# A two-layer decoder step: squares summed on TensorE, the root taken from PSUM, smaller residual chunks and stores

## The reference

```python
def rmsnorm(x, g):
    y = x * lax.rsqrt(jnp.mean(x * x, axis=-1, keepdims=True) + RMS_EPS)
    return y * g

def layer(x, g_pre, g_post, w_in, w_o, ...):
    h = rmsnorm(x, g_pre)
    ... = jnp.split(h @ w_in, SPLITS, axis=-1)      # mixer inputs, memory queries, gate
    o = jnp.concatenate([o_tok, o_mem], axis=-1)
    y = (o * jax.nn.silu(gate)) @ w_o
    return x + rmsnorm(y, g_post)
```

## Time and profile before

| | |
|---|---|
| time, three runs | 1710.7, 1711.69, 1712.37 us; median 1711.69 |
| profiled execution, its own time | 1713.43 us |
| its span, first to last instruction | 1711.8 us |
| busy: PE, DVE, ACT, POOL | 1623.2, 1049.7, 401.3, 160.8 us |
| mean granted TensorE clock | 0.981 of 2.4 GHz |
| transfers | 419.95 MB |

### The profile page before, as it was taken

How to read it: one execution, slowest core, us unless ns; L and a number is a source line. 1 busy time by engine, 2 the same in 40 slices (tenths; PEclk the granted TensorE clock), 3 DMA queues, 4 the chain that set the end, 5 groups by cost and what they waited for, 6 DMA issues and landing times.

```text
span 1711.8 us, 27852 instructions
## 1 busy us (share of the span) xinstructions
PE 1623.2 (95%) x9596; PEld 1285.7 (75%) x9596; DVE 1049.7 (61%) x4973; ACT 401.3 (23%) x1002; POOL 160.8 (9%) x295
## 2 busy tenths in 40 slices
PE   7999999899999999989989989999999999999995
PEld 6677776677777777657977867777777777888895
DVE  4887546746465555437872467777777777431755
ACT  2131111101121212211111433333333333221011
POOL 1121112112111121220000000000000000020000
PEclk9999999999999999999999999999999999999998
DMA  9689999999999999995433233333333323374441
GB/s 384 235 335 415 411 406 395 384 396 420 405 401 422 417 419 412 366 379 239 148 141 149 103 101 102 103 103 102 103 109 103 103 78 118 111 272 176 148 148 52
DMA packets 101725, 419.95 MB, mean 245 GB/s; under 512 B 41796, under 2 KB 46288, under 8 KB 91984
## 3 DMA queue, kind: packets, MB, share of 16 engines
q0 software_dynamic: 41680, 218.91, 32.1%
q1 hardware_dynamic: 53256, 187.54, 28.9%
q10 hardware_dynamic: 6648, 11.73, 1.8%
HBM read 405.28 MB, written 12.85 MB: 244 GB/s over the span
## 4 chain that ended last, share of the span: by engine, by line
PE 76%; DVE 9%; ACT 6%; DMA 5%; issue 2%; POOLq 0%; POOL 0%; ACTq 0%; DVEq 0%; SPq 0%
PE psum L743 25%; PE psum L1171 11%; PE psum L812 10%; PE psum L794 6%; PE psum L1034 5%; DMA kvr<-in_cv 3%; PE psum L732 3%; PE psum L781 2%; PE psum L1218 2%; DMA kvr<-in_ck 1%; PE psum L1228 1%; PE psum L754 1%; ACT gT L1777 1%; PE psum L769 1%; DVE kvr L1939 1%
## 5 line engine op out<-in xcount | busy, mean ns | idle before, releaser
L1939 DVE CUSTOM_DVE_ANT_0 kvr<-kvr,arena 128x128 f32<-128x128 f32 x1488 | 323.6, 285 | 114.4 <-DMA kvr<-in_ck 114.0
L743 PE MATMUL psum<-hT,wring 128*128 128x264 f32 x1536 | 364.8, 394 | 0.0
L743 PEld LDWEIGHTS psum<-hT,wring 128*128 128x128 f32 x1536 | 291.9, 194 | 67.8 <-issue 19.8
L1171 PE MATMUL psum<-hT,kvr 128*128 128x264 f32 x1152 | 283.0, 391 | 1.8 <-DVE hT L2267 1.8
L1171 PEld LDWEIGHTS psum<-hT,kvr 128*128 128x128 f32 x1152 | 213.5, 191 | 42.3 <-issue 8.9
L794 PE MATMUL psum<-hT,kvr 128*128 128x264 f32 x512 | 121.5, 388 | 0.0
L1939 DVE DVE_READ_ACCUMULATOR2_ANT arena<- 128x1 f32 x1488 | 120.2, 81 | 0.0
L794 PEld LDWEIGHTS psum<-hT,kvr 128*128 128x128 f32 x512 | 94.8, 190 | 15.8 <-issue 0.9
L677 POOL DMA_DIRECT2D kvr<-in_cv x128 | 67.7, 529 | 377.9 <-PE psum L1034 288.2
L1034 PE MATMUL psum<-kvr,arena 128*32 128x384 f32 x1024 | 98.8, 502 | 4.5 <-DMA kvr<-in_cv 4.5
L677 POOL DMA_DIRECT2D kvr<-in_ck x128 | 67.6, 528 | 216.7 <-issue 216.7
(11 more groups left out here) (433 smaller groups left out, 2318.5 us busy)
## 6 DMA issues: line engine op xcount, KB each, us to landing
kvr<-in_ck POOLq DMA_DIRECT2D x128, 768.0 KB, 11.8
kvr<-in_cv POOLq DMA_DIRECT2D x128, 768.0 KB, 11.4
kvr<-in_wrkv SPq DMA_DIRECT2D x12, 3072.0 KB, 11.9
kvr<-in_wo SPq DMA_DIRECT2D x14, 2048.0 KB, 8.3
wring<-in_wkv SPq DMA_DIRECT2D x12, 2048.0 KB, 11.8
wring<-in_wm SPq DMA_DIRECT2D x8, 2048.0 KB, 12.5
wring<-in_wg SPq DMA_DIRECT2D x8, 2048.0 KB, 12.0
kvr<-in_wg SPq DMA_DIRECT2D x8, 2048.0 KB, 8.8
```

Source lines behind the costliest of these rows:

```text
L743: last = mm(psum[:, m % 2, 0:n], w[:, k, t * P:(t + 1) * P], rhs[:, k, 0:n], start=(k == 0), stop=(k == KT - 1))
L1171: last = mm(psum[:, m % 2, 0:T], w[:, k, t * P:(t + 1) * P], hT[:, k, :], start=(k == 0), stop=(k == KT - 1))
L1939: last = v_.tensor_tensor_reduce(page, page, qb[:, n % 2, h * P:(h + 1) * P], 1.0, 0.0, ALU.mult, ALU.add, S[:, n % 2, j * FH + h:j * FH + ...
```

## The change

- **Squares.** DVE adds the squares of rows j = 0 to 13 only. PE adds the accumulator and the last two squares, straight from ACT's buffers, in one accumulation over three ones-products (`n_sq` counts the two squares). This holds in both layers.
- **Root.** ACT takes the root from PSUM with scale 1/D and a bias of RMS_EPS from the new tile `eps`; DVE takes the reciprocal after it, not before. A Sqrt of one column ahead of row 14 loads ACT's function table there. `rsx` now lies in `acc0`.
- **Joint.** `residual` runs over eight chunks of 1, 1, 2, 2, 2, 4, 2 and 2 rows; the weighted sums of row 15 come after the fifth. ACT counts `h_out` for every row, and PE waits for every row. The other three ones-products follow LoRA's row 13. LoRA writes banks 6 and 7, so queries 0 and 1 wait for no LoRA eviction. `hT` is scaled by `inv2` quarter by quarter as PE has read it for the last query (`q_read`), ahead of that query's eviction.
- **End.** PE puts rows 0 to 6 of `xT` into seven banks by an identity product and adds the scaled rows of `oT` to them; ACT copies the sums back. DVE only scales these rows and does both passes for rows 7 to 15. SP issues seven stores of 2, 2, 3, 3, 3, 2 and 1 rows in that order.

Left out of the diff: the weight buffers of the late products count on the semaphores `g_full` instead of `u_full` (with matching numbers).

```diff
@@ -273,6 +273,7 @@
+        eps = sb("eps", [P, 2])
@@ -373,7 +374,7 @@
-        rsx = sq0[:, 0, :]
+        rsx = acc0
@@ -462,15 +463,23 @@
+        RESIDUAL = [(0, 1), (1, 2), (2, 4), (4, 6), (6, 8), (8, 12), (12, 14), (14, 16)]
+        SUMS_LEFT = 5
+        ADDED = [(0, 2, True), (2, 4, True), (4, 7, True), (7, 10, False), (10, 13, False), (13, 15, False), (15, 16, False)]
+        ADD_BANKS = (0, 1, 3, 4, 5, 6, 7)
 @@ -604,7 +613,7 @@
             unit(I["wqm1"], 1, 0)
-            sp.wait_ge(sem("h_out"), 16)
+            sp.wait_ge(sem("h_out"), 28)
             for j in range(2):
@@ -657,6 +666,11 @@
                 late_unit(v)
+            x_added, x_out = 0, 0
+            for k0, k1, on_pe in ADDED:
+                x_added, x_out = (x_added + k1 - k0, x_out) if on_pe else (x_added, x_out + 1)
+                sp.wait_ge(*(sem("x_added"), x_added) if on_pe else (sem("x_out"), x_out))
+                sp.dma_start(O["yT"][:, k0 * T:k1 * T], xT[:, k0:k1, :].rearrange("p k t -> p (k t)")).then_inc(sem("stored_y"), 16)
@@ -755,20 +769,21 @@
-            def lora_tiles(after):
+            def lora_tiles():
                 pe.wait_ge(sem("w_full0"), 32)
-                for t in range(2):
-                    pe.wait_ge(sem("p_free"), M_LORA + t + 1)
+                pe.wait_ge(sem("y_out"), 2 * FEW0)
                 for k in range(KT):
-                    if k % 4 == 0:
-                        pe.wait_ge(sem("h_out"), after + k // 4 + 1)
+                    pe.wait_ge(sem("h_out"), 8 + k + 1)
                     for t in range(2):
-                        m = M_LORA + t
                         w = wring[:, 0, t * KT * LORA:(t + 1) * KT * LORA].rearrange("p (k n) -> p k n", k=KT)
-                        last = mm(psum[0:LORA, m % 2, 0:T], w[:, k, :], hT[:, k, :], start=(k == 0), stop=(k == KT - 1))
+                        last = mm(psum[0:LORA, 6 + t, 0:T], w[:, k, :], hT[:, k, :], start=(k == 0), stop=(k == KT - 1))
                         if k == KT - 1:
                             last.then_inc(sem("p_done"), 1)
+                    if k == KT - 3:
+                        for n, (out, total) in enumerate(((B, accg), (Wp, accx), (Xp, accxx))):
+                            pe.wait_ge(sem("n_acc"), min(n + 4, 5))
+                            mm(out[:, 0:T], ones, total, start=True, stop=True).then_inc(sem("n_ss"), 1)
@@ -776,9 +791,11 @@
                     w = wring[:, slot, :].rearrange("p (k n) -> p k n", k=KT)
-                    pe.wait_ge(sem("p_free"), m + 1)
+                    pe.wait_ge(sem("p_free"), m + 1 if t >= 2 else M_LORA + 2)
                     for k in range(KT):
                         last = mm(psum[:, m % 2, 0:T], w[:, k, t % 2 * P:(t % 2 + 1) * P], hT[:, k, :], start=(k == 0), stop=(k == KT - 1))
+                        if t == 3 and k in (3, 7, 11):
+                            last.then_inc(sem("q_read"), 1)
                     last.then_inc(sem("p_done"), 1)
@@ -1139,10 +1156,13 @@
                 few_products(i)
-            for n, (out, total) in enumerate(((A, acc0), (B, accg), (Wp, accx), (Xp, accxx))):
-                pe.wait_ge(sem("n_acc"), min(n + 3, 5))
-                mm(out[:, 0:T], ones, total, start=True, stop=True).then_inc(sem("n_ss"), 1)
-            lora_tiles(8)
+            pe.wait_ge(sem("n_acc"), 3)
+            mm(A[:, 0:T], ones, acc0, start=True, stop=False)
+            for n in range(2):
+                pe.wait_ge(sem("n_sq"), 2 + n + 1)
+                last = mm(A[:, 0:T], ones, sq0[:, n, :], start=False, stop=n == 1)
+            last.then_inc(sem("n_ss"), 1)
+            lora_tiles()
             memory_queries()
@@ -1166,7 +1186,7 @@
                     if o == -2 and t == 0:
-                        pe.wait_ge(sem("h_out"), 12 + n + 1)
+                        pe.wait_ge(sem("h_out"), 24 + n + 1)
                     for k in range(4 * (n % 4), 4 * (n % 4) + 4):
@@ -1389,7 +1409,18 @@
             pe.wait_ge(sem("n_acc"), 6)
-            mm(A[:, 0:T], ones, acc1, start=True, stop=True).then_inc(sem("n_ss"), 1)
+            mm(A[:, 0:T], ones, acc1, start=True, stop=False)
+            for n in range(2):
+                pe.wait_ge(sem("n_sq"), 4 + n + 1)
+                last = mm(A[:, 0:T], ones, sq1[:, n, :], start=False, stop=n == 1)
+            last.then_inc(sem("n_ss"), 1)
+            pe.wait_ge(sem("y_out"), 2 * (FEW0 + 8))
+            for n, bank in enumerate(ADD_BANKS):
+                mm(psum[:, bank, 0:T], ident, xT[:, n, :], start=True, stop=False)
+            for n, bank in enumerate(ADD_BANKS):
+                chunk = [k0 <= n < k1 for k0, k1, _ in ADDED].index(True)
+                pe.wait_ge(sem("y_normed"), chunk + 1)
+                mm(psum[:, bank, 0:T], ident, oT[:, n, :], start=False, stop=True).then_inc(sem("p_done"), 1)
@@ -1423,7 +1454,9 @@
                     act.wait_ge(sem("sq_used"), nth - 1)
-                ac(sq[:, j % 2, :], oT[:, n, :], ACT.Square)
+                last = ac(sq[:, j % 2, :], oT[:, n, :], ACT.Square)
+                if j >= 14:
+                    last.then_inc(sem("n_sq"), 1)
                 ac(oT[:, n, :], oT[:, n, :], ACT.Copy, scale=gpost(layer)[:, n:n + 1]).then_inc(sem("p_free"), 1)
@@ -1628,16 +1661,16 @@
             for n in range(16):
+                if n == 14:
+                    ac(eps[:, 1:2], eps[:, 1:2], ACT.Sqrt)
                 output_tile(0, n)
+            act.wait_ge(sem("n_ss"), 3)
+            ac(rsx, A[:, 0:T], ACT.Sqrt, scale=1.0 / D, bias=eps[:, 0:1]).then_inc(sem("n_rt"), 1)
+            for n, (k0, k1) in enumerate(RESIDUAL):
+                act.wait_ge(sem("x_new"), n + 1)
+                for k in range(k0, k1):
+                    ac(hT[:, k, :], xT[:, k, :], ACT.Copy, scale=gpre(1)[:, k:k + 1]).then_inc(sem("h_out"), 1)
             act.wait_ge(sem("n_ms"), 3)
-            ac(rsx, inv2, ACT.Sqrt).then_inc(sem("n_rt"), 1)
-            for c in range(4):
-                act.wait_ge(sem("x_new"), c + 1)
-                for k in range(4 * c, 4 * c + 4):
-                    last = ac(hT[:, k, :], xT[:, k, :], ACT.Copy, scale=gpre(1)[:, k:k + 1])
-                last.then_inc(sem("h_out"), 1)
-            act.wait_ge(sem("n_ms"), 4)
             ac(inv2, inv2, ACT.Sqrt).then_inc(sem("n_rt"), 1)
@@ -1794,13 +1827,15 @@
             for n in range(16):
+                if n == 14:
+                    ac(eps[:, 1:2], eps[:, 1:2], ACT.Sqrt)
                 output_tile(1, n)
-            root(4, rs1)
-            for c in range(4):
-                act.wait_ge(sem("x_out"), c + 1)
-                act.dma_start(O["yT"][:, 4 * c * T:(4 * c + 4) * T], xT[:, 4 * c:4 * c + 4, :].rearrange("p k t -> p (k t)"))\
-                    .then_inc(sem("stored_y"), 16)
-            act.wait_ge(sem("stored_y"), 64)
+            act.wait_ge(sem("n_ss"), 7)
+            ac(rs1, A[:, 0:T], ACT.Sqrt, scale=1.0 / D, bias=eps[:, 0:1]).then_inc(sem("n_rt"), 1)
+            for n, bank in enumerate(ADD_BANKS):
+                act.wait_ge(sem("p_done"), M_WO1 + 16 + n + 1)
+                ac(xT[:, n, :], psum[:, bank, 0:T], ACT.Copy).then_inc(sem("x_added"), 1)
+            act.wait_ge(sem("stored_y"), 16 * len(ADDED))
             act.wait_ge(sem("stored_lf"), 16)
@@ -2105,7 +2140,7 @@
                     joined(i)
-                for j in (14, 15):
+                for j in () if layer else (14,):
                     output_sums(layer, j)
@@ -2127,12 +2162,15 @@
                 s, total = (sq0, sq1)[layer][:, j % 2, :], (acc0, acc1)[layer]
-                last = v_.tensor_copy(total, s) if j == 0 else tt(total, total, s, ALU.add)
+                if layer or j < 14:
+                    last = v_.tensor_copy(total, s) if j == 0 else tt(total, total, s, ALU.add)
                 if layer:
...
                     dve.wait_ge(sem("sq_used"), nth + 1)
+                    if j == 13:
+                        dve.sem_inc(sem("n_acc"), 1)
                     return
-                if j == 15:
+                if j == 13:
                     last.then_inc(sem("n_acc"), 1)
@@ -2150,12 +2188,13 @@
-            def residual(c, buf):
-                rows4 = slice(4 * c, 4 * c + 4)
-                ch.do(tt(oT[:, rows4, :], oT[:, rows4, :], buf.unsqueeze(1).to_broadcast([P, 4, T]), ALU.mult))
-                return tt(xT[:, rows4, :], xT[:, rows4, :], oT[:, rows4, :], ALU.add)
+            def residual(k0, k1, buf):
+                rows_ = slice(k0, k1)
+                ch.do(tt(oT[:, rows_, :], oT[:, rows_, :], buf.unsqueeze(1).to_broadcast([P, k1 - k0, T]), ALU.mult))
+                return tt(xT[:, rows_, :], xT[:, rows_, :], oT[:, rows_, :], ALU.add)
+            v_.memset(eps[:, :], RMS_EPS)
             quad, total = oT[:, 0:4, :], oT[:, 4:8, :]
@@ -2223,16 +2262,16 @@
-            dve.wait_ge(sem("n_ss"), 3)
-            ch.do(ts(inv2, A[:, 0:T], 1.0 / D, RMS_EPS, ALU.mult, ALU.add))
-            v_.reciprocal(inv2, inv2).then_inc(sem("n_ms"), 1)
```

(44 more changed lines are left out.)

## The result

The changed kernel took 1698.27 us, the median of five runs (1692.97 to 1701.55), and the kernel before 1710.7 in the five runs beside them (1706.42 to 1712.37). The ratio is 0.9922 with a 95% interval of 0.9902 to 0.9941: **13.3 us faster (10.1 to 16.8)**, where the prediction had 10.7. Applied to the 1710.7 of the same runs, the ratio gives 1697.4, a hair under the range's low end of 1697.5. The direction was right, and so were the terms of the two edited places; the gain came out 2.6 larger than forecast, although 10.7 still lies inside the interval.

The account below looks back on a forecast made before the run. PE carries three quarters of the chain; changes off it pay only where PE stands still. Joint 6.7 plus end 4.0 gave 10.7 off the 1711.69 median: 1701.0 us, range 1697.5 to 1706.5.

Parts of the forecast that it names:

- the terms of the two edited places: Between the layers and at the kernel's end: 6.7 and 4.0 us saved, sum 10.7.
- The joint: Between the layers: LoRA's earlier end 4.5, no eviction wait 0.45, hT scaling hidden 1.75; sum 6.7 us.
- that case: LoRA between the layers: the clock returns to full rate more slowly, costing 1.7 us.
- The end: Last rows: earlier reciprocal 1.41, less DVE work 1.77, smaller last store 0.85; sum 4.0 us.
- Two signs of being wrong: Clock at 0.50 past 896 in LoRA; third SP store issued after the fourth's rows are ready.
- Rival 1: LoRA between the layers: PE pauses between rows and stays at half rate; net 3.4 us slower, 1715; chance 0.06.
- Rival 2: Turn loop waits for something not shifted, so the joint's gain stays there and only the end pays: 1707.7; chance 0.09.
- Rival 3: At the end, PE at half rate makes the additions hold up the stores: net 5.2 us faster, 1706.5; chance 0.09.
- Rival 4: Table reload costs 0.9 at each root, one or two further half-rate stretches in the turn loop: 1709 to 1712; chance 0.06.
- The step that failed: Turn loop from 945 to 1693: the joint's shift of 6.7 us runs through unchanged.
- the half rate in the first turn: Stretch after 987 in the turn loop: its absence, worth 3.2 us, served to widen the range.

Follow-up runs that it names:

- fill: Changed kernel plus eight unread products of ones in PE's pause ahead of LoRA; one run, joint gains 0.05 us.
- the joint alone: Changed kernel with the end of the kernel before; r at 51.35 against 58.13 us, loop 747.30.
- the end alone: Kernel before with only the end changed; end 14.49 against 18.40 us, loop 751.04.
- last three: Changed kernel with its last two stores made one of three rows; DVE done 0.26 us earlier, span ends 0.20 later.
- DVE adds all: Changed kernel with DVE doing both passes for all sixteen rows at the end; the additions on PE and ACT are worth 2.4 to 2.5 us.
- turn filler: Changed kernel plus five unread products in PE's waits in the first turn; first turn 1.63 us shorter, loop 746.65 against 746.37.
- all three: Changed kernel plus unread products ahead of LoRA and in the first turn, and row 15's sums later; ratio 0.9903 to the kernel before.
- sums late: Changed kernel with only row 15's weighted sums two chunks later on DVE; one run, queries 0.58 us later.
- no early load: Changed kernel without the one-column Sqrt ahead of row 14, both layers; 1698.22 us in a single run, 0.9 lost in each place.
- chunks of four: Changed kernel with the residual in four chunks of four rows, row 15's sums after the second; queries start at 25.81, 2.94 us later.
- fill and sums late: Changed kernel plus eight unread products ahead of LoRA and row 15's sums two chunks later; ratio 0.9930 to the kernel before.
- scaled after: Changed kernel with hT scaled after the last query's eviction, as before; queries to r 30.43 us instead of 28.48.

## Where the prediction held, and the step that failed

**The joint held, term by term.** Counted from the mark: PE's sum of row 15 ended at 1.53 (forecast 1.62), the reciprocal began at 2.13 (2.07), LoRA at 5.56 (5.45), queries at 22.87 (22.7), r at 51.35 (51.4). Two small errors cancelled: the queries started 4.76 earlier than before, not 4.95, and from there to r it took 2.02 less, not 1.75 (removing the scaling was worth 1.95 by itself). The root from PSUM took 0.49, not the 0.39 of the earlier trace rows; unlike that one it reads a column, the bias. That the column is the reason was not tested, but ACT's copies that read a column of `gvec` took 0.50 beside 0.42 for its squares, which read none. The prices of two- and three-row passes (0.15 + 0.277 per row) came out at 0.70 and 0.97 as worked out. There is some luck in the agreement: with the longer fall, which two of the five profiled kernels with this joint and no fill ahead of it had, r comes 0.9 later. The prediction priced that case at 1.7.

**The end held.** The last addition came at 12.18 (forecast 12.07). The last store landed in 1.9 (taken: 1.8, bounds 1.6 and 2.65).

**Two signs of being wrong came up** without the mechanism failing. Half rate in LoRA lasted until 9.8 after the mark, where the sign was 9.1 (896); since DVE and PE tie there, that cost at most 0.05, as the fill shows. And the third store *was* issued after the fourth's rows were ready (1693.93 against 1693.46), at a cost of about 0.1: the last store was issued at 1697.57, 0.03 after DVE's last pass, and landed in 1.9, against 1.8 where the stores stood further apart.

**The rivals.** Rival 1 (PE never warm) did not happen: half rate lasted 3.4 us in LoRA. The rule of the Trainium skill that spoke for it ("TensorE: Matmul & The Clock Gate", A second HAM failure mode) needs short pauses between groups of products, and this case hardly tests it: PE had none in LoRA (13.10 of 13.10 us busy after the rise), and the clock fell once and rose once. Rival 2 falls by the joint alone. Rival 3 did not come up: PE kept full rate at the end. Rival 4's reload would have stood between row 15 and the root; the trace has its only load there at 876.21, and removing that load cost 0.9, as forecast for a reload. Its two falls in the turn loop did not come in this execution, but they did in the end alone (6.8 and 3.4 us at half rate, loop 751.04).

**The step that failed** is "From 945 the chain is PE's turn loop with inputs that it releases itself, so I let the shift run through to 1693". It put the loop's own change at nothing. In the profiled pair the loop gave 2.00: 1.25 in the first turn and the rest in later turns, of which most take 41.81 and three of before about 42.1. The prediction saw the half rate in the first turn, priced its absence at 3.2, and used it only to widen the range.

What the runs showed in its place: the loop has no fixed length; it goes, with some overlap, with the time that the clock is at 0.50 in it. Over the fourteen profiles:

```
half rate in the loop   profiles   loop               of them
none                    4          745.78 to 746.65   fill, last three, turn filler, all three
3.4 us                  5          746.05 to 747.30   after, joint only, sums late, no early load, chunks of four
6.8 us or more          5          747.69 to 751.04   before, end only, fill and sums late, scaled after, DVE adds all
```

The profiled execution of before had 6.8 us, that of the change 3.4. In the first turn alone, 34.69 to 39.29 over all profiles, the two kernels with the turn filler had the clock at 1.00 and took 34.70 and 34.69, 1.6 less than the profiled change and 2.9 less than before; two without it had no fall there either (fill 34.70, last three 35.04).

**What stays open.** How the 2.6 of the medians divide is not shown. Three things enter. One is the loop. Another is the base: the prediction subtracted from 1711.69, and the kernel before took 1710.7 in the runs beside. The third is the work ahead of the joint, which is all but the same in all kernels and which the prediction left out of its range: the mark came anywhere between 877.99 and 890.67. That too goes with the clock: the traces show 20.5 us at half rate ahead of the mark in the six profiles with the mark at 882.32 or before, and 23.9 to 40.9 us in the eight with a later one. Of the change's five runs two (1692.97 and 1693.3, mean granted clock 0.993) lie 5 to 8.6 us below the other three (0.988 to 0.990). They left no trace; a first turn without half rate is worth 1.6 and can't be all of it.

Whether the change itself makes the fall in the first turn rarer, or the runs met it less often, can't be told either: the two profiled kernels without the new joint had 37.58 and 39.29, those with it 34.69 to 38.11, which overlap. The steps of up to 1.0 in later turns have no cause shown.

## What to carry to other kernels

Count segments from one instruction that both kernels share: with terms of 0.1 to 2 us in a kernel whose executions differ by 8, the segments agreed to 0.1 wherever the clock fell alike, and the total could not. Look up where the clock falls before comparing: the same joint came out 0.9 longer by that alone. Where a stage downstream holds a stretch at half rate, don't price its change at nothing: its length is a term with several values. Products read by nothing, put into the first turn's pauses, kept the clock up in both kernels that had them, but later parts of the loop took the gain back, once whole and once for the most part, so follow such a gain to the end of the kernel. When two engines tie, speeding up one gains nothing (0.05 us here) until the other is relieved too (1.34).

## What the runs showed of the hardware

PE's clock fell at different points of the same pause of 4.0 us. In the profiled change it stayed at 1.00 through the pause and fell 0.8 us after work resumed; in the kernels "last three" and "DVE adds all" it fell 1.6 and 1.5 us before work resumed. Either way the products behind the pause paid: 3.4 us at half rate in the first, 5.2 and 5.3 in the others. Square after Sqrt on ACT showed no table load (one load at 876.21, then Sqrt, two rows of squares and copies, and the root). A load of 1.28 us was followed by the root 0.01 later. Stores of 132, 264 and 396 KB from SP landed in 1.8, 2.0 and 2.4 us where they stood 0.8 to 1.9 us apart; closer together, those of 396 KB took up to 3.1.
